# Bidirectional encoder layer on eight cores: two more input buffers for the gated merge, the second sequence's first loads placed in the last unit of the first, more output buffers

## The reference: what is computed

```
x = x + 0.5 * SwiGLU_1(RMSNorm(x))                     # width 2816
h = RMSNorm(x)
qA,kA,vA, qB,kB,vB, gates = h @ W_in
oA = DifferentialAttention(qA,kA,vA)   # 8 heads, full length, ALiBi, two softmaxes
oB = WindowedGQA(qB,kB,vB,sink)        # 16 query heads, |t-s| <= 128
y  = sig(gA) * (oA @ P_A) + sig(gB) * (oB @ P_B)
x = x + y @ W_out
x = x + 0.5 * SwiGLU_2(RMSNorm(x))
out = RMSNorm_final(x)
```

## Time and profile before

| | |
|---|---|
| runs | 3912.71, 3914.57, 4577.05 us, median 3914.57 us |
| profiled execution | 3922.39 us, span of its slowest core (core 2) 3921.3 us |
| spans of cores 0 to 7 | 3913.1, 3916.0, 3921.3, 3907.9, 3900.1, 3897.9, 3906.9, 3907.2 us |
| TensorE busy (core 2) | 3795.2 us, 97% |
| VectorE, ScalarE, GpSimd busy | 62%, 46%, 7% |
| bytes moved | 657.68 MB, mean 168 GB/s |
| granted TensorE clock, mean of a core | 0.988 to 0.994 |

### The profile page before, as it was taken

The page is one execution under the profiler, slowest core; times in us unless marked ns, Lnnn a source line. Parts: engine busy times, 40 slices in busy tenths (PEclk is TensorE's granted clock), DMA queues, the critical chain, the costliest instruction groups (busy, mean ns, idle before and its releaser), DMA issues.

```text
span 3921.3 us, 83279 instructions; the slowest of 8 cores (3897.9 to 3921.3 us)
## 1 busy us (share of the span) xinstructions
PE 3795.2 (97%) x28860; PEld 2163.5 (55%) x29321; DVE 2422.0 (62%) x5477; ACT 1800.6 (46%) x2672; POOL 262.0 (7%) x385
## 2 busy tenths in 40 slices
PE   8999999999999999998999999999999999999998
PEld 3444455666566666565665566566555544444443
DVE  5445243678878677875567767768877644353533
ACT  3422022666666666664565556556655512121211
POOL 1010000000111100100000000000000000000000
PEclk9999999999999999999999999999999999999999
DMA  9968797766777876765856655655644486576554
GB/s 198 208 137 203 161 234 197 166 166 160 183 182 179 176 164 151 169 160 121 183 157 160 158 143 155 167 137 155 178 130 135 141 218 179 155 198 177 183 156 130
DMA packets 410791, 657.68 MB, mean 168 GB/s; under 512 B 168800, under 2 KB 272480, under 8 KB 409568
## 3 DMA queue, kind: packets, MB, share of 16 engines
q1 hardware_dynamic: 384848, 546.15, 51.4%
q0 software_dynamic: 24960, 105.13, 14.8%
q10 hardware_dynamic: 576, 1.05, 0.1%
HBM read 570.29 MB, written 160.79 MB: 186 GB/s over the span
## 4 chain that ended last, share of the span: by engine, by line
PE 85%; DVE 4%; issue 4%; ACT 3%; DMA 3%; SPq 1%; DVEq 0%; ACTq 0%; POOL 0%; POOLq 0%
PE bank L388 85%; SPq L416 1%; DMA qS<-qs_d 1%; ACT pc L391 0%; DMA ra_69<-s_gu 0%; ACT et_107 L391 0%; DMA R_62<-x 0%; ACT et_105 L391 0%; DMA od_d<-obf 0%; DVE R_62 L397 0%; ACT et_109 L391 0%; DMA ra_68<-s_pp 0%; DMA oTa<-od_d 0%; DVE et_105 L394 0%; DMA R_61<-x 0%
## 5 line engine op out<-in xcount | busy, mean ns | idle before, releaser
L388 PE MATMUL bank<-qS,kS 64*128 64x192 bf16 (+1 forms) x1024 | 251.5, 246 | 19.1 <-DMA qS<-qs_d 19.1
L391 ACT ACTIVATE et_108<-bank 128x1024 bf16<-128x1024 f32 x171 | 174.8, 1022 | 199.6 <-PE bank L388 199.6
L391 ACT ACTIVATE et_106<-bank 128x1024 bf16<-128x1024 f32 x171 | 174.8, 1022 | 183.0 <-PE bank L388 182.6
L391 ACT ACTIVATE et_110<-bank 128x1024 bf16<-128x1024 f32 x170 | 173.8, 1022 | 174.4 <-PE bank L388 174.2
L388 PE MATMUL bank<-H_63,ra_67 128*128 128x512 bf16 x923 | 218.3, 382 | 6.2 <-DVE H_63 L397 2.9
L388 PE MATMUL bank<-H_63,ra_66 128*128 128x512 bf16 x903 | 215.6, 384 | 6.7 <-DVE H_63 L397 2.8
L388 PE MATMUL bank<-H_63,ra_68 128*128 128x512 bf16 x873 | 207.6, 382 | 11.3 <-DVE H_63 L397 4.1
L388 PE MATMUL bank<-H_63,ra_69 128*128 128x512 bf16 x873 | 206.5, 382 | 7.3 <-DMA ra_69<-s_gu 3.1
L394 POOL TENSOR_TENSOR rs_127<-ms_126,mhalf 128x2 f32<-128x2 f32 x128 | 106.1, 829 | 1600.6 <-DVE ms_126 L397 1326.1
L388 PE MATMUL bank<-H_63,ra_70 128*128 128x512 bf16 x879 | 205.6, 380 | 3.8 <-issue 0.8
L388 PE MATMUL bank<-qD_96,kD 64*128 64x256 bf16 x2048 | 176.9, 273 | 0.5 <-issue 0.5
(11 more groups left out here) (367 smaller groups left out, 8260.5 us busy)
## 6 DMA issues: line engine op xcount, KB each, us to landing
ra_69<-s_gu SPq DMA_DIRECT2D x56, 512.0 KB, 4.2
ra_68<-s_gu SPq DMA_DIRECT2D x55, 512.0 KB, 4.3
ra_67<-s_gu SPq DMA_DIRECT2D x55, 512.0 KB, 4.3
ra_66<-s_gu SPq DMA_DIRECT2D x55, 512.0 KB, 4.5
ra_70<-s_gu SPq DMA_DIRECT2D x54, 512.0 KB, 4.0
rd_71<-s_d SPq DMA_DIRECT2D x52, 352.0 KB, 3.2
rd_73<-s_d SPq DMA_DIRECT2D x52, 352.0 KB, 3.4
rd_72<-s_d SPq DMA_DIRECT2D x48, 352.0 KB, 3.2
```

The source lines that it names most:

```text
L388: self.S.add("pe", lambda e: e.matmul(out, lhsT=lhsT, rhs=rhs, start=start, stop=stop), r=r, w=w)
L391: self.S.add("act", lambda e: e.activation(out=out, in_=in_, func=func, **kw), r=r, w=w)
```

## The change

It touches where inputs lie and when they are loaded; every engine's arithmetic is the same work.

- **Room for P's inputs.** `oAa`, `oAb` lie in the region of `aT0` (the activations between GU and D), which is idle in phase 2 from D7 of phase 1 to GU0, and from D3 to GU4. P1 and P5 take a and b from there, P7 takes h, a and b from `px`. So P1's transposes are listed in W(6,7)'s last chunks, P2's a and b after P0, P5's after D3, P6's a and b after P4, P7's after P5. P4's a and b are listed about 22 slots earlier in each unit. `pace` (2 or 3 chunks for one transpose) takes the place of `hurry`.
- **The second sequence's start.** In the last unit of the first sequence `b_qk` and `b_av` now list the first half of qS and kS, the local table sw, half of vS, and both q tiles of the second sequence. `first_loads` of the second keeps kD and vD (10 chunks ahead of the first slot, was 12) and the second half of qS, kS and vS (6 chunks behind it, was 2 ahead). For the first sequence qS, sw and qD are listed ahead of kD, vD and td.
- **Buffers.** `obf` 1 to 2, `obs` 2 to 3; the td ring is 256 columns shorter, and two of its pieces are listed 4 slots later in each unit.
- **Norm pieces.** In P two pieces a chunk where a second norm is queued; in the urgent stretches TensorE's piece runs ahead of each chunk.

```
-NTD = NM + 1024
+NTD = NM + 768
...
         self.aT = [sb("aT0", [128, NFF, TB], BF16, keys=([("aT", 0, f) for f in range(NFF)], 1024))]
+        for i, t in enumerate("ab"):
+            setattr(self, "oA" + t, sb("oA" + t, [128, 8, TB], BF16, at=self.ptr - 22528 + 8192 * i, keys=([("oA" + t, c) for c in range(8)], 1024)))
...
-        self.obf = sb("obf", [128, 2, 128], BF16)
+        self.obf = [sb("obf%d" % i, [128, 2, 128], BF16, keys=("obf", i)) for i in range(2)]
...
-        self.obs = [sb("obs%d" % i, [128, 2, 128], BF16, keys=([("obs", i, j) for j in range(2)], 256)) for i in range(2)]
+        self.obs = [sb("obs%d" % i, [128, 2, 128], BF16, keys=([("obs", i, j) for j in range(2)], 256)) for i in range(3)]
...
-        if self.dq[2] and n - self.doled[1] >= (1 if self.hurry else 2):
+        if self.dq[2] and n - self.doled[1] >= self.pace:
             self.doled[1] = n
-            for _ in range(min(len(self.dq[2]), 2 if self.hurry else 1)):
-                self.dq[2].pop(0)[1]()
+            self.dq[2].pop(0)[1]()
...
-    def pin(self, t, x):
-        if x:
+    def pin(self, t, b):
+
+        if b == 7:
             return self.px[t], ("px", t)
+        if b in (1, 5) and t != "h":
+            return {"a": self.oAa, "b": self.oAb}[t], ("oA" + t,)
         return {"h": (self.H[1], ("H", 1)), "a": (self.oTa, ("oTa",)), "b": (self.oTb, ("oTb",))}[t]
...
         if part == 0:
+            if sq == 0:
+                self.load_S(0, 0, 0)
+                self.load_sw(0)
+                self.load_qD(0, 0, 0)
             self.load_kD(sq, 0, 0)
-            self.load_qD(sq, 0, 0)
             self.load_vD(sq, 0, 3)
...
         else:
-            self.load_S(sq, 0, 0)
-            self.load_sw(0)
-            for k in range(2):
-                self.load_vS(sq, 0, k)
-            self.load_qD(sq, 0, 1)
+            if sq == 0:
+                self.load_vS(0, 0, 0)
+                self.load_qD(0, 0, 1)
+            self.load_vS(sq, 0, 1)
             self.load_S(sq, 0, 1)
...
-            if self.urgent:
+            if self.urgent or (self.twice and len(self.bg) > 1):
                 self.post()
...
+        nxt = (sq, u + 1) if u < 7 else (1, 0) if sq == 0 else None
...
+        if nxt:
+            if l == 4:
+                self.load_sw(nxt[1])
+            if l == 17:
+                self.load_S(*nxt, 0)
         if l % 8 == 7:
             if l < 16:
                 self.load_qD(sq, u, l // 8 + 2)
-            elif u < 7:
-                self.load_qD(sq, u + 1, l // 8 - 2)
+            elif nxt:
+                self.load_qD(*nxt, l // 8 - 2)
...
-                          15: [(v + 1, 1536, 2048)], 23: [(v + 1, 2048, 2560)], 31: [(v + 1, 2560, 3072)]}.get(l, ()):
+                          19: [(v + 1, 1536, 2048)], 27: [(v + 1, 2048, 2560)], 31: [(v + 1, 2560, 3072)]}.get(l, ()):
...
-        if l == 19 and u < 7 and u % 2:
-            self.load_vS(sq, (u + 1) // 2, 0)
+        if l == 19 and u % 2 and (u < 7 or sq == 0):
+            self.load_vS(*((sq, (u + 1) // 2) if u < 7 else (1, 0)), 0)
...
         def f3():
+            self.ofn += 1
+            k = self.ofn % 2
...
     def evac_S(self, i, sq, u, n, src):
-        oi = n // 2 % 2
+        self.obn += 1 - n % 2
+        oi = self.obn % 3
...
-            marks[a - (16, 12)[q]] = lambda q=q: self.first_loads(q, 0)
-            marks[a - (8, 2)[q]] = lambda q=q: self.first_loads(q, 1)
+            marks[a - (16, 10)[q]] = lambda q=q: self.first_loads(q, 0)
+            marks[a + (-8, 6)[q]] = lambda q=q: self.first_loads(q, 1)
...
-                self.hurry = k == "O" and b0 == 0
+                self.twice = k == "P"
...
                     self.load_p(0, "h")
+                    self.load_p(1, "ab")
...
-                if done < want or len(self.gset) > 2:
+                if done < want or len(self.gset) > 2 or self.urgent:
                     self.pre()
...
-                while self.p4 < min(8, (self.slot - 4) // 32):
+                while self.p4 < min(8, (self.slot - 14) // 32 + 1):
...
                         if q:
-                            self.load_p(4, "ab", range(self.p4, 8))
-                            self.flush(("p", 4))
-                            self.load_p(5)
-                            self.p4 = 8
+                            assert self.p4 == 8
...
-        if k == "P" and b < 7:
-            if b != 4:
-                self.load_p(b + 1, "h" if b == 3 else "hab")
+        if k == "P":
+            if b in (0, 3, 4):
+                self.load_p(b + 1, "h")
+            if b == 0:
+                self.load_p(2, "ab")
+                self.pace = 3
+            if b == 1:
+                self.load_p(2, "h")
+            if b == 2:
+                self.load_p(3)
             if b == 3:
                 self.p4 = 0
+            if b == 4:
+                self.load_p(6, "ab")
+            if b == 5:
+                self.load_p(6, "h")
+                self.load_p(7)
+        if (k, b) == ("D", 3):
+            self.load_p(5, "ab")
+            self.pace = 2
+        if (k, b) == ("O", 4):
+            self.pace = 3
```

More of the change, by code:

```diff
@@ L308, in decl_chip @@
         self.vD = sb("vD", [128, 8, 2, 2, 129], BF16, keys=([("vD", k) for k in range(8)], 1032))
-        self.td = sb("td", [128, NTD + 256], BF16, keys=([("td", j) for j in range(41)], 256))
+        self.td = sb("td", [128, NTD + 256], BF16, keys=([("td", j) for j in range(39)], 256))
         self.qS = sb("qS", [128, SEQ], BF16, keys=([("qS", k) for k in range(2)], 2048))
@@ L319, in decl_chip @@
         self.of = sb("of", [128, 2, 128], F32, keys=([("of", q) for q in range(2)], 512))
-        self.obf = sb("obf", [128, 2, 128], BF16)
+        self.obf = [sb("obf%d" % i, [128, 2, 128], BF16, keys=("obf", i)) for i in range(2)]
         self.osq = sb("osq", [128, 2, 128], F32)
-        self.ssv.append(sb("ssv1", [128, 4, 4, 65], BF16, at=self.ptr - 2560, keys=("ssv", 1)))
+        self.ssv.append(sb("ssv1", [128, 4, 4, 65], BF16, at=self.ptr - 3072, keys=("ssv", 1)))
         self.ssv.append(ssv2)
-        self.obs = [sb("obs%d" % i, [128, 2, 128], BF16, keys=([("obs", i, j) for j in range(2)], 256)) for i in range(2)]
+        self.obs = [sb("obs%d" % i, [128, 2, 128], BF16, keys=([("obs", i, j) for j in range(2)], 256)) for i in range(3)]
         self.rc2 = sb("rc2", [128, 2], F32)
@@ L365, in decl_chip @@
         self.dn_ = 0
+        self.ofn = self.obn = 0
         self.eti = {}
@@ L701, in load_p @@
         for t in what:
-            dst, dk = self.pin(t, b == 5)
+            dst, dk = self.pin(t, b)
             if t == "h":
@@ L851, in st_P @@
     def st_P(self, b):
-        x = b == 5
-        H, hk = self.pin("h", x)
+        H, hk = self.pin("h", b)
         for c in range(8):
@@ L866, in st_P @@
                 bb, bk = self.bank(True)
-                src, nm = self.pin("ab"[s], x)
+                src, nm = self.pin("ab"[s], b)
                 self.gemm8(bb, bk, wp[:, s], wpk, src, nm)
@@ L1100, in b_qk @@
         self.part.append(rest)
[L1101 to L1110, removed]
+        nxt = (sq, u + 1) if u < 7 else (1, 0) if sq == 0 else None
+        if u < 7:
+            if l == 2:
+                self.load_kD(sq, u + 1, 0)
+            if l == 29:
+                self.load_kD(sq, u + 1, 1)
+            if l == 31:
+                self.load_S(sq, u + 1, 1)
+        if nxt:
[3 more added lines that the diff above has]
+                self.load_S(*nxt, 0)
         if l % 8 == 7:
@@ L1191, in f3 @@
         def f3():
+            self.ofn += 1
+            k = self.ofn % 2
             for q in range(2):
-                self.stt(self.obf[:, q, :], self.of[:, q, :], self.rs2[:, q:q + 1], self.gsub, ALU.mult, ALU.mult,
-                         [("of", q), "rs2", "gsub"], ["obf"])
+                self.stt(self.obf[k][:, q, :], self.of[:, q, :], self.rs2[:, q:q + 1], self.gsub, ALU.mult, ALU.mult,
+                         [("of", q), "rs2", "gsub"], [("obf", k)])
             t0 = sq * SEQ + qb * 256
-            self.dma(self.od_d[u, t0:t0 + 256, :].rearrange("(q p) e -> p q e", p=128), self.obf, ["obf"],
-                     [("od", u, 8 * sq + qb)], ("otd", 0))
+            self.dma(self.od_d[u, t0:t0 + 256, :].rearrange("(q p) e -> p q e", p=128), self.obf[k], [("obf", k)],
+                     [("od", u, 8 * sq + qb)], ("otd", k))
         self.later += [(i, f1), (i + 1, f2), (i + 2, f3)]
     def evac_S(self, i, sq, u, n, src):
-        oi = n // 2 % 2
+        self.obn += 1 - n % 2
+        oi = self.obn % 3
         obs = self.obs[oi][:, n % 2, :]
```

## The result

The changed kernel took 3878.8 us (median of 3875.6, 3876.26, 3881.33 and 3884.57) where the kernel before took 3913.64 (median of 3905.98, 3912.71, 3914.57 and 4577.05); the ratio is 0.9919, with a 95% interval of 0.9897 to 0.9941. The forecast was 3878, range 3852 to 3904.

What follows compares the result with a forecast made beforehand. TensorE's instruction order was taken as the bound, leaving its waits and low clock to win. Core 2's 36.6 us of waits plus 13 of clock gave 3872.8; core 1, ending last, 3888.8 profiled; medians 3874 to 3881, forecast 3878, range 3852 to 3904.

Steps and rivals of the forecast that it cites:

- The second start: Start of the second sequence: TensorE's wait for qS goes, 14.8 us on core 2 and 10.6 on core 1.
- The empty stretch: 1790 to 1805 us, DMA share 0.16: the second sequence's first loads were to go there, some 50 us earlier.
- The norm pieces: Waits for H_63: 2.9 us go in W(6,7) and 2.0 in GU1; the other 4.9 stay.
- The first start: Start of the first sequence: 2.2 of core 2's 4.3 us for qS go, the rest becomes another wait in that line.
- P's inputs: Core 2: P1's wait for oTb, 4.1 us, and GU5's waits for weights, 5.1 us, go.
- The wait for a weight that the prediction calls P5's: TensorE's 3.5 us wait for a weight stays, since P5's transposes stay beside the same loads.
- The one obf: VectorE's wait for obf's store: with two buffers the 5.5 us TensorE waits for es_113 on core 2 go.
- Which core ends last: Core 1 was to end last, with its 5.15 us wait for nh in phase 1 untouched.
- Core 1's span: Forecast to fall by 28.3 us, 19.3 of waits and 9 of clock, from 3916.0 to 3887.7.
- The 126 us of standing still: Time TensorE stands still, start and end included, taken as what can be won besides the lower clock.
- The clock: Each place where a wait goes also wins 2 us that TensorE lost at the lower clock behind it.
- Rivals D and E: D: td ring has too little slack, 3960 us, chance 0.05. E: P1's loads come when they came, 3914, chance 0.05.

Runs made afterwards that it cites:

- e1: Changed kernel with only the second sequence's first loads put back where they were; ratio 0.9956 to the kernel before, gain 19.2 us.
- e4: Changed kernel with P's inputs loaded as before the change; ratio 0.9934 to the kernel before, gain 29.0 us.
- e9: Changed kernel with the first sequence's first loads in the old order; ratio 0.9922 to the kernel before, gain 29.4 us.
- e8: Changed kernel with first td pieces listed right after setup and block 5's residual held through P4 and O4; ratio 0.9898 to the kernel before.
- e11: Kernel before with two obf and nothing else; ratio 0.9996 to the kernel before, gain 0.2 us.
- e2: Changed kernel with one obf in place of two; ratio 0.9929 to the kernel before, gain 32.2 us.
- a2: The changed kernel run again, unaltered; ratio 0.9915 to the kernel before, mean core span 3865.4 us.
- e3: Changed kernel with the norm pieces as before the change; gain 24.0 us over the kernel before, no interval recorded.
- e5: Changed kernel with one obf, the longer td ring and td pieces at their old slots; ratio 0.9923 to the kernel before, gain 33.0 us.
- e12: Changed kernel with block 5's residual held back through P4 and O4, nothing else; ratio 0.9906 to the kernel before, gain 35.0 us.

## Why the prediction was right, and where its steps failed

**The second start** was the largest term and right: 14.8 forecast on core 2 and 10.6 on core 1, each with 2 to 2.5 of clock; 11.1 us of waits and 14.6 of time came back as a mean (e1). The empty stretch that the prediction named is not where the loads went: they stand some 100 us earlier, at a share of 0.59, and that was enough.

**The norm pieces**: 4.9 and two places of clock, 8.9, were forecast, 9.8 measured. I had left GU1's second and third waits (0.9 each on core 2) where they were; they went too.

**The first start**: half was forecast to go, the other half to turn into a wait for something else in the line. It is so, with the name not forecast: ScalarE waits for a free sq buffer whose store stands in SyncE's line. Mean 4.6 to 2.6, and on four cores only.

**P's inputs** were mis-sized: 4.1 and 5.1 us of waits with 2 of clock at each, some 13, were taken from core 2; the part is worth 4.8 in the mean of the cores (e4), since most cores waited less there. The wait for a weight that the prediction calls P5's is one of P4 (its row multiplies oTa). It was to stay, and it did not: no core of the changed kernel's profile has it, and waits for O4's weight (up to 2.8 us there, 6.8 in e9) and block 5's h stand behind it, so that the place still has 1.9 in the mean. e8 shows that these hang on the residual's loads beside the transposes.

By the Trainium skill (Advanced Engine Details and Errata, "X-Bar Transpose (TRN2)") transposing loads are as fast as regular ones. In SyncE's line they were not in any trace here: 1.1 us each at best and 1.1 to 1.2 in the median, against 0.32 for a weight. From issue to landing the trace agrees: median 4.5 us for oTa's on core 2 before, 4.6 for kD's plain loads, of the same 128 KB. And the long holds of the earlier trace rows are not the transposes' own: the pair above took 2.38 without the residual beside it.

**The one obf** is the step that failed: "With two, the store has until the next but one output. The 5.5 us go." They went, but not by the second buffer. Two buffers alone gained 0.2 (e11), one buffer in the changed kernel lost 1.6 (e2), both within the noise. I take the 5.5 us for an accident of that execution, in which core 2 met a late store at the wrong moment; its profile is the only one of the kernel before as it was. Why just then, and what the waits put down to issue are, stays open.

**Which core ends last** failed too: core 1 was to be last with its nh wait untouched; it was first, at 3857.5. That wait is none of core 1's: it was 2.5 on core 4, 3.1 on core 7 in a2, 4.8 on core 3 in e1. What made core 1 late in the profile before was for the most part no wait at all. Its granted clock there is 0.81, between TensorE's two levels, in 20 stretches of 4 to 7 us, with TensorE busy ahead of each; eight matmuls that took 1.89 us ahead of one take 2.27 in it, so here a value between the levels is not a window that holds both. By an estimate (0.19 of their 104.9 us) that is 19.7 us on cores 0 and 1; cores 2 and 3 have 11 such stretches, 9.6 us, cores 4 to 7 none. One of core 1:

```profile
2728.20:2735.60 7.40, 7.40 (x68) 4.54 (x67) 6.62 (x16) 4.84 (x8) 1.29 (x2) 0.81 0.96 285
```

Core 1's span fell by 58.5 us, where 28.3 were forecast. So that 3878 met 3878.8 is in part luck. The sum was taken from a core that ended first, and from the span of a stretch of time in which its clock was low; its 28.3 came near the mean gain of the cores, 33.8, while core 2's 49.6 held the waits of obf and P that most cores lack. The 126 us of standing still were over-read too: core 2's profile lacks 461 matmuls, and core 1, with all of them, stood still for 69.0 (3916.0 - 3847.0). No term rests on that.

**The clock** at 2 us a place held. Half of the time at 0.50 behind a wait is lost: by an estimate from the granted clocks of the eight cores 1.5 us in the mean in W(6,7) and 2.3 in GU1 (e3), and 2.6 behind the longer wait of e1. With the waits that is 5.4 + 3.8 = 9.2 of e3's 9.8 and 11.1 + 2.6 = 13.7 of e1's 14.6.

**Rivals D and E** fall too. With the old td ring and slots the gain is 33.0 (e5), without them 32.2 (e2), and no engine waits for td once attention runs. P1's transposes are issued from 1963 to 2045 us on core 2, ahead of O0 at 2056, and no core waits for oAa or oAb in P1.

The parts, each undone alone, make 14.6 + 9.8 + 4.8 + 4.4 + 1.6 = 35.2 of the 33.8 us measured together. With an uncertainty of 3 to 4 us in each, that shows no more than that nothing large is missing.

## What to carry to other kernels

A load that the next stage starts with belongs in a stretch where the DMA engines have room (a share of 0.59 was enough here), not in the line in which everything else for that stage stands: the line stayed full (1.01) and nobody waited. Take the terms of a sum from all cores, not from the slowest of one execution: a wait that two cores have and six don't may be an accident, and a core can be slow by its clock (19.7 us here) and not by its waits. A second buffer pays only where the first one's wait reaches the engine that sets the time.

## What was not expected of the hardware

The wait that is left at the first start falls on one core of each pair (0 and 1, 2 and 3, 4 and 5, 6 and 7). In the changed kernel's profile it is 5.9, 4.8, 4.4 and 5.7 us on cores 0, 2, 4 and 6 and absent on 1, 3, 5 and 7; in e4 the long ones fall on 1, 2, 5 and 7, in e12, of cores 4 to 7, on 4 and 7. The spared core ends about 10 us sooner, as the spans above show. In the kernel before every core waited for qS there. It looks as if the two cores of a pair shared something that is short in that stretch, but no run here separates it.

The stretches at 0.81 come in pairs as well. In the profile before, cores 0 and 1 have the same 20 and cores 2 and 3 the same 11, each within 0.3 us of the other core's when each is counted from its own start, but the two pairs have different ones; in the changed kernel's profile cores 4 and 5 share 6, and cores 6 and 7 another 6 (5.9 us lost on each). What sets them is not shown. Core 0's, beside core 1's above:

```profile
2728.40:2735.80 7.40, 7.40 (x56) 4.02 (x53) 5.64 (x14) 5.17 (x8) 0.00 (x0) 0.81 0.78 179
```
